# ScalarE copies the gelu tile into PSUM and rounds there, VectorE multiplies the gates in place: an expert layer on one Trainium2 core

## The reference, cut to what matters

```python
top_s, pos = lax.top_k(cand, PEER_TOPK)
expert_idx = jnp.take_along_axis(cand_idx, pos, axis=-1)
gate = jax.nn.softmax(top_s, axis=-1)
u = expert_u[expert_idx]
act = jax.nn.gelu(jnp.einsum('thkd,td->thk', u, hc).astype(jnp.float32), approximate=False)
vv = expert_v[expert_idx]
return jnp.einsum('thk,thkd->td', (gate * act).astype(hc.dtype), vv)
```

## Time and profile before

| | |
|---|---|
| median of 3 runs | 2557.08 us (2556.6 to 2558.24) |
| profiled execution, own time | 2565.91 us |
| its span | 2564.1 us |
| instructions | 37409 |
| VectorE busy | 1939.3 us (76%) |
| ScalarE busy | 802.4 us (31%) |
| POOL busy | 1343.4 us (52%) |
| the pairs | 1494 to 2553 us of the span |

### The profile page before, as it was taken

The page is one execution under the profiler, slowest core; times in us unless marked ns, Lnnn a source line. Parts: engine busy times, 40 slices in busy tenths (PEclk is TensorE's granted clock), DMA queues, the critical chain, the costliest instruction groups (busy, mean ns, idle before and its releaser), DMA issues.

```text
span 2564.1 us, 37409 instructions
## 1 busy us (share of the span) xinstructions
PE 2434.5 (95%) x13120; PEld 2168.8 (85%) x13120; DVE 1939.3 (76%) x3539; ACT 802.4 (31%) x1217; POOL 1343.4 (52%) x1185
## 2 busy tenths in 40 slices
PE   7999999999999999999989989999999899999998
PEld 6885888888888877888978888998889899889998
DVE  5476633322799867699999968888888978888787
ACT  3145222222322437233445522222222222222222
POOL 4520565666555551653300056767667776667553
PEclk9999999999999999999999999999999999999999
DMA  4211232232222231222346777777767777677553
GB/s 167 93 45 34 74 112 93 98 106 100 98 98 98 82 101 41 86 99 74 107 156 233 266 212 245 237 257 249 255 227 232 256 241 259 227 254 231 175 161 102
DMA packets 210870, 402.72 MB, mean 157 GB/s; under 512 B 118336, under 2 KB 123840, under 8 KB 207424
## 3 DMA queue, kind: packets, MB, share of 16 engines
q1 hardware_dynamic: 64224, 233.36, 27.3%
q0 software_dynamic: 27648, 100.68, 10.7%
q10 hardware_dynamic: 118880, 67.18, 8.8%
HBM read 369.25 MB, written 31.92 MB: 156 GB/s over the span
## 4 chain that ended last, share of the span: by engine, by line
PE 64%; DVE 26%; issue 5%; POOL 3%; ACT 1%; DMA 1%; DVEq 0%; POOLq 0%; ACTq 0%; SPq 0%
PE bank L1760 20%; PE bank L1762 19%; PE bank L1761 19%; DVE bank L1659 8%; POOL lo L593 3%; DVE ohg L1629 2%; DVE lo L1568 1%; DVE xT L1674 1%; DVE oh L1625 1%; DVE oh L1626 1%; PE bank L1918 1%; PE bank L1929 1%; PE bank L1905 1%; DVE idx L1527 1%; DVE inH L1095 1%
## 5 line engine op out<-in xcount | busy, mean ns | idle before, releaser
L593 POOL TENSOR_TENSOR lo<-raw,hi 128x256 fp32r<-128x256 f32 (+1 forms) x950 | 1140.1, 1230 | 1083.3 <-ACT hi L679 562.1
L1760 PE MATMUL bank<-inH,hi 128*128 128x512 f32 (+1 forms) x2112 | 793.4, 376 | 18.5 <-DVE inL L1096 13.6
L1761 PE MATMUL bank<-inL,hi 128*128 128x512 f32 (+1 forms) x2112 | 784.5, 371 | 0.0
L1762 PE MATMUL bank<-inH,lo 128*128 128x512 f32 (+1 forms) x2112 | 784.4, 371 | 0.0
L1760 PEld LDWEIGHTS bank<-inH,hi 128*128 128x128 f32 x2112 | 398.4, 189 | 68.4 <-issue 17.7
L1760 PE MATMUL bank<-WH,hi 128*128 128x416 f32 x1024 | 368.3, 360 | 71.4 <-DVE xT L1674 63.4
L1762 PEld LDWEIGHTS bank<-inH,lo 128*128 128x128 f32 x2112 | 398.2, 189 | 44.1
L1761 PEld LDWEIGHTS bank<-inL,hi 128*128 128x128 f32 x2112 | 398.6, 189 | 42.7 <-issue 0.2
L1674 DVE TENSOR_TENSOR xT<-xT,bank 128x416 f32<-128x416 f32 x504 | 292.3, 584 | 153.1 <-PE bank L1762 125.2
L679 ACT ACTIVATE hi<-raw 128x1024 fp32r<-128x1024 f32 x232 | 243.7, 1056 | 406.9 <-PE bank L1762 395.7
L1761 PE MATMUL bank<-WL,hi 128*128 128x416 f32 x1024 | 363.7, 355 | 0.0
(11 more groups left out here) (323 smaller groups left out, 2837.2 us busy)
## 6 DMA issues: line engine op xcount, KB each, us to landing
raw<-stream SPq DMA_DIRECT2D x440, 512.0 KB, 3.3
Gd<-gates ACTq DMA_DIRECT2D x32, 832.0 KB, 5.7
gates<-stage_a ACTq DMA_DIRECT2D x13, 1024.0 KB, 4.3
gates<-stage_b ACTq DMA_DIRECT2D x13, 1024.0 KB, 4.8
tbl<-gqa ACTq DMA_DIRECT2D x8, 384.0 KB, 3.2
spilled<-res ACTq DMA_DIRECT2D x12, 208.0 KB, 4.0
A<-spilled ACTq DMA_DIRECT2D x6, 416.0 KB, 3.4
xT<-x SPq DMA_DIRECT2D x4, 512.0 KB, 8.9
```

Source lines behind the costliest of these rows:

```text
L593: ins = pool.tensor_tensor(lo[:, r, part], raw[:, r, part], hi[:, r, part].bitcast(F32), ALU.subtract)
L1760: pe.matmul(bank, wh, xh, start=start, stop=False)
L1761: pe.matmul(bank, wh, xl, start=False, stop=False)
L1762: return pe.matmul(bank, wl, xh, start=False, stop=stop_)
```

## The change

ScalarE copies each gelu tile from `A` into the staging bank (`move`, semaphore `a_moved`). VectorE's product then reads the staging bank and `Gd` and writes the staging bank in place (`gate_done`). ScalarE makes the high part from the staging bank (`high_w_part`, semaphore `high_w`), and VectorE's `low_part` waits for it. On VectorE `high_part` is gone and the order in `weigh_and_add` is another. In the long pairs ScalarE's copy for pair j + 1 stands right behind the gelu of pair j; in the short ones it stands behind the `hi` of the pair before. The rounding of both halves follows. Line numbers from here on in the changed kernel: product L1689, copy L1030, rounding L1035, gelu L1046, `hi` L1020.

```diff
+            def move(j, e):
+
+                if j > HEAD:
+                    act.wait_ge(gelu_done, min(A_TILES + 2 * (j - 1) + (e + 1), 2 * N_PAIRS))
+                else:
+                    act.wait_ge(gelu_done, 2 * j + (e + 1))
+                if 0 < j < HEAD or j > N_BOTH:
+                    act.wait_ge(w_done, 2 * (j - 1) + (e + 1))
+                act.activation(staged(j, e), A[:, (2 * j + e) % A_TILES, :], ACT.Copy).then_inc(a_moved, 1)
+
+            def high_w_part(j, e):
+
+                act.wait_ge(gate_done, 2 * j + (e + 1))
+                act.activation(WH[:, j % 2, e, :DT], staged(j, e), ACT.Copy).then_inc(high_w, 1)
+
...
                     act.activation(A[:, (2 * j + e) % A_TILES, :], B[6 + e][:, :DT], ACT.Gelu).then_inc(gelu_done, 1)
+                    move(j + 1, e)
                     high_peer(j, e, S_MAIN // RING + 2)
...
+                for e in (0, 1):
+                    high_w_part(j + 1, e)
                 act.wait_ge(y_done, j * KD + KD)
...
             act.wait_ge(spill_out, 16 * N_SPILLED)
+            for e in (0, 1):
+                move(0, e)
+            for e in (0, 1):
+                high_w_part(0, e)
             for j in range(HEAD):
...
+                for e in (0, 1):
+                    move(j + 1, e)
+                for e in (0, 1):
+                    high_w_part(j + 1, e)
                 act.wait_ge(y_done, (j + 1) * KD)
...
             def gated(j, e):
...
-                a = A[:, (2 * j + e) % A_TILES, :].rearrange("p (b t) -> p b t", t=SPILL)
-                chain(dve.tensor_tensor(stage(j, e).rearrange("p (b t) -> p b t", t=SPILL), a, Gd[:, buf, :, 2 * (j % 2) + e, :], ALU.mult))
+                dve.wait_ge(a_moved, j * 2 + (e + 1))
+                a = staged(j, e).rearrange("p (b t) -> p b t", t=SPILL)
+                dve.tensor_tensor(a, a, Gd[:, buf, :, 2 * (j % 2) + e, :], ALU.mult).then_inc(gate_done, 1)
...
-                weigh(j, 0)
+                gated(j, 0)
                 add(last, 0)
                 add(last, 1)
+                low_part(j, 0)
                 gated(j, 1)
                 add(last, 2)
-                high_part(j, 1)
                 add(last, 3)
                 low_part(j, 1)
```

More of the change, by code:

```diff
@@ L488, in program @@
         acc_added = sem("acc_added")
+        a_moved = sem("a_moved")
+        gate_done = sem("gate_done")
+        high_w = sem("high_w")
         ident = cs[:, CC["ident"]:CC["ident"] + P]
@@ L503, in by_token, with staged @@
             return v[:, 2 * (m % 2):2 * (m % 2) + 2, n // 2 * 2 * P:(n // 2 + 1) * 2 * P]
+        def staged(j, e):
+            return B[(4 if j < HEAD else 6) + e][:, :DT]
         def gain(name, k=0):
@@ L1061, in _ @@
                     load_gates(j // 2 + 1, (j // 2 + 1) % 2)
+                if j + 1 < N_PAIRS:
+                    for e in (0, 1):
+                        move(j + 1, e)
+                    for e in (0, 1):
+                        high_w_part(j + 1, e)
                 n = S_LAST + 2 * (j - N_BOTH)
@@ L1643, in _ @@
             assert u == BUILT
-            def stage(j, e):
-                return B[(4 if j < HEAD else 6) + e][:, :DT]
             def gated(j, e):
@@ L1652, in gated @@
                 dve.wait_ge(g_loaded[buf], 16 * (j // 4 + 1))
[L1653 to L1657, removed]
-                a = A[:, (2 * j + e) % A_TILES, :].rearrange("p (b t) -> p b t", t=SPILL)
-                chain(dve.tensor_tensor(stage(j, e).rearrange("p (b t) -> p b t", t=SPILL), a, Gd[:, buf, :, 2 * (j % 2) + e, :], ALU.mult))
-            def high_part(j, e):
-                chain(dve.tensor_scalar(WH[:, j % 2, e, :DT], stage(j, e), 1.0, None, ALU.mult))
-            def low_part(j, e):
[L1665 to L1670, removed]
+                dve.wait_ge(a_moved, j * 2 + (e + 1))
+                a = staged(j, e).rearrange("p (b t) -> p b t", t=SPILL)
+                dve.tensor_tensor(a, a, Gd[:, buf, :, 2 * (j % 2) + e, :], ALU.mult).then_inc(gate_done, 1)
+            def low_part(j, e):
+                dve.wait_ge(high_w, j * 2 + (e + 1))
+                dve.tensor_tensor(WL[:, j % 2, e, :DT], staged(j, e), WH[:, j % 2, e, :DT].bitcast(F32), ALU.subtract).then_inc(w_done, 1)
             def add(j, k):
@@ L1738, in weigh_and_add @@
                     fold_in(SETS - 1)
-            weigh(0, 0)
-            weigh(0, 1)
+            for e in (0, 1):
+                gated(0, e)
+            for e in (0, 1):
+                low_part(0, e)
             for j in range(1, N_PAIRS):
```

## The result

| | before | after |
|---|---|---|
| median | 2556.84 us (4 runs, 2555.39 to 2558.24) | 2482.61 us (4 runs, 2480.68 to 2485.88) |
| profiled execution, own time | 2565.91 us | 2480.68 us |
| its span | 2564.1 us | 2478.8 us |

The ratio is 0.9706, 95% interval 0.9693 to 0.9718. That is 74 us less between the medians and 85 us between the two profiled executions. The forecast was 2477 us, in a range of 2470 to 2502.

What follows compares the result with a forecast made beforehand. TensorE, 95% busy, was taken as the bound, its losses blamed on held-up products. -80.8 - 3.6 + 4.3 = -80.1 us took the profiled 2565.9 to 2485.8, and 8.8 lower for the median gave 2477, range 2470 to 2502.

Steps and rivals of the forecast that it cites:

- The mechanism: Expert stage: POOL holds VectorE's two-SBUF product, delaying the add that frees TensorE's bank; reading PSUM makes it 0.59 us.
- the sum: Whole kernel: -80.8 for the long stretch, -3.6 for the first mixes, +4.3 at the start, together -80.1 us.
- The five first mixes: Mixes from 1494.45 to 1546.10 us: 3.6 us lost to one stretched product would be won back.
- The start: Before the first mix: the first copy stands behind the wait for the last spilled tile, costing 4.3 us.
- the 80.8 us: Long stretch, 1546.10 to 2396.94 us: 850.8 us taken for 770.0 of TensorE work, the loss to vanish.
- The step that failed: From profile to median: the profiled 2565.9 us less 80.1, then the median taken 8.8 us lower, giving 2477 us.
- The spare of the short pairs: First 5 and last 16 mixes: add of k=2 done at M+5.85, wanted at M+6.8 (M: mix start), 0.9 us spare.
- new wait: Long pairs: a transfer or POOL comes late at 18.1 us a pair, giving 2490 to 2502 or 2519 us; chance 0.12.
- ScalarE wasn't late in the short pairs: Rival, short pairs: copy and product at 1.0 us each would cost 0.4 us in 21 pairs, 2485 us; chance 0.05.
- the slower side: Short pairs: the product still held by POOL's subtractions, kernel slower at 2583 or 2620 us; chance 0.03.
- The difference between row and rule: Product beside POOL: a profile row shows it waiting for two subtractions, the Trainium skill says one instruction; 2620 against 2583 us.
- the spreads of `h`: Three operations also reading two SBUF tensors might be held up by POOL, within the TensorE-bound range up to 2484 us.

Runs made afterwards that it cites:

- third profile of the change: The changed kernel run again without any edit, its third profile: 2483.62 us, ratio 0.9708 to the kernel before, span 2486.9 us.
- second profile: The kernel before, unchanged, run and profiled once more: 2559.07 us (one run), span 2557.2 us.
- product-only kernel: Against the kernel before, ScalarE copies and the product is made in place in the staging bank, but VectorE keeps the rounding: 2498.28 us, ratio 0.9751.
- pieces: The kernel before with each of POOL's subtractions in the pairs cut into four of 256 columns: 2478.64 us, ratio 0.9668.

## Why the prediction was right, and where it was off

**The mechanism** was right in what it says of the product and of the bank behind it. The product reads one SBUF tensor and isn't held (594 ns against 0.59 us forecast); copies take 515 ns and roundings 512 (0.52 each); the long stretch fell to TensorE's pace. In the third profile of the change, at 9.04 us a group like the kernel before, the long groups sum to 380.64 + 379.79 us and the turns to 10.2, 770.6 against 770.0 forecast: 80.2 us less where the sum has 80.8. The five first mixes are 3.6 less, as in the sum. The start costs 4.0 to 4.1 us more idleness, against 4.3.

**What the 80.8 us were made of** the prediction had wrong. It put all of it down to waiting for held-up products, but the earlier trace rows shows 61.6 us of waits. Idle time was 62.0 us. The other 18.8 stand in TensorE's busy time, 788.8 us where the work is 770.0. Of these 10.2 are the six times at the lower clock. The rest stands in the matmuls right before and behind each wait, which count longer there: 0.34 us and 0.30, where the usual step from one to the next is 0.19. The long stretch of the change in its third profile has almost nothing of either:

```profile
1548.40:2319.05 770.65, 770.27 (x4130) 765.57 (x4129) 506.48 (x801) 298.11 (x431) 583.43 (x360) 1.00 0.81 270
```

None of the ten profiles of kernels without these 41 waits shows the lower clock anywhere in the long stretch. So that part went away with the waits, and the sum came out right although it didn't know the term: that is luck. In the first mixes too, 1.8 us of the 3.6 were a wait, and 1.7 a time at the lower clock.

**The step that failed** is "The median of the runs lies 8.8 lower, 2557.1, and I take the same difference from it". The lost time was counted in one profiled execution, and that one had spent more time at the lower clock than most: 6.3 us more lost than in the kernel's second profile, nearly all of it by the clock, which the sum put at nothing behind the start. The earlier trace rows had it, as a granted clock of 0.99. What a run of the kernel before hasn't lost, the change can't give back. With the second profile's losses, 76.1 in the long stretch and 2.0 in the first mixes against 80.8 and 3.6, the same sum is 76.1 + 2.0 - 4.3 = 73.8, and from 2557.1 it gives 2483.3; 2482.6 was measured. This is worked out after the fact, and no record shows the clock of the three runs behind that median. That the two first profiles differ by 85 and not by 80 has another cause, the 7.0 us of faster pace of one run.

**The spare of the short pairs** was named by the wrong add. I gave 0.9 us for the add of k = 2; the add of k = 0 is due 2.3 us earlier and had 0.65 (3.85 against 4.5). For the change it made no difference. For the product-only kernel it was the mistake in the expectation, 11 us.

**The rivals.** No new wait came in the long pairs: at a DMA share of 0.82 (0.81 forecast) POOL and the gathers kept up. ScalarE wasn't late in the short pairs. The product wasn't held any more, so the slower side had nothing to stand on. The difference between row and rule on which that rival's price hung is still there: pieces obey the rule, nearly always, and pairs of long subtractions didn't. One thing that the prediction named did come in part: two of the six operations of the spreads of `h`, which still read two SBUF tensors (now L1739), took 2.89 us where none took over 0.99 before. TensorE didn't wait for them.

**What I had not put among the ways it could be read:** that the gain needs neither ScalarE nor PSUM. The page's views pointed at the product, and I followed its operand. The order of time from which the earlier trace rows is cut held the other reading as well: the tile of the second product is ready 0.8 us into the mix, and POOL comes a good second later.

## What to carry to other kernels

When an operation of one engine is stretched only while another engine works, first see when it could run instead and how long the other's instructions are: one moved call and one smaller piece size each gave here what 256 new instructions on a third engine gave. When lost time is counted as length minus work, split it into idle time and time at a lower granted clock, and take a second profile before the sum goes against the median of other runs. And when a wait is put in front of a chain of steps, list every due time behind it, not the last alone.

## What the runs showed of the hardware

- VectorE's product of two SBUF tensors, 0.59 us alone, took 3.1 to 5.7 us in 41 of the 42 long pairs, through two of POOL's subtractions in a row (1024 columns each), also where its record begins 0.2 to 0.5 us ahead of POOL's. With subtractions of 256 columns, 125 of 128 products ended within 1.2 us.
- Beside the same subtractions, operations with one SBUF and one PSUM input weren't stretched: 600 ns at most in 128 products.
- ScalarE writes 416 fp32 columns from SBUF into PSUM in 515 ns, and rounds them from PSUM into SBUF in 512.
- TensorE does the same matmuls of 416 columns at 0.1867 or at 0.1884 us each, at the same granted clock of 1.00, by run and stretch: 8.96 or 9.04 us for 48.
- After 5 as after 12 us without a matmul TensorE's next ones come 0.35 to 0.49 us apart, at a granted clock of 0.50, the level of 1.2 GHz, as in the earlier trace rows.
- In the kernel before the granted clock also fell to 0.50 for 3.4 us at a time behind some of TensorE's waits of 2.1 to 2.7 us, seven times in one profile of the pairs and four times in another, at 1.7 us of lost work each.
